# Compressing cached rows with the rows as stationary operand and 256 columns of weights moving, two slots an item

## What is computed

```python
def compress(rows, pe, w1, w2):
    L = rows.shape[1]
    n_cmp = (L - CMP_LEN) // CMP_STRIDE + 1          # CMP_LEN 32, CMP_STRIDE 16
    idx = np.arange(n_cmp)[:, None] * CMP_STRIDE + np.arange(CMP_LEN)[None, :]
    blk = rows[:, idx] + pe[None, None, :, None, :]
    h = jax.nn.gelu(jnp.einsum('bnlgd,lde->bnge', blk, w1))
    return jnp.einsum('bnge,ef->bngf', h, w2)
```

## Time and profile before

| what | value |
|---|---|
| three runs | 2734.03, 2746.77, 2745.37 us, median 2745.37 |
| profiled execution | 2739.43 us, span 2737.6 us |
| mean granted TensorE clock | 0.796 of 2.4 GHz |
| TensorE matmul busy | 2034.7 us (74%) |
| VectorE busy | 1263.8 us (46%) |
| DMA | 963.81 MB, mean 352 GB/s |
| queue of the gathers (software) | 627.05 MB, 56.5% of the 16 engines' span |
| queue of SyncE's loads (hardware) | 332.46 MB, 32.4% |

### The profile page before, as it was taken

The page is one execution under the profiler, slowest core; times in us unless marked ns, Lnnn a source line. Parts: engine busy times, 40 slices in busy tenths (PEclk is TensorE's granted clock), DMA queues, the critical chain, the costliest instruction groups (busy, mean ns, idle before and its releaser), DMA issues.

```text
span 2737.6 us, 30582 instructions
## 1 busy us (share of the span) xinstructions
PE 2034.7 (74%) x10278; PEld 1228.5 (45%) x10278; DVE 1263.8 (46%) x2362; ACT 326.5 (12%) x747; POOL 786.7 (29%) x594
## 2 busy tenths in 40 slices
PE   8999999779989989859998455464544459883334
PEld 5777666434478967647776112211210016540000
DVE  0500112341046775767786354325343454787551
ACT  0000110420021010010010021002010020011011
POOL 0000000000002143433344243225252474346662
PEclk9999999989999989979999766785766555555555
DMA  9789888965327599999999999999999999999997
GB/s 401 294 342 362 350 312 340 384 230 205 122 104 283 178 376 383 370 364 392 387 378 379 351 360 412 406 358 411 389 402 422 422 421 421 422 413 401 422 422 292
DMA packets 213165, 963.81 MB, mean 352 GB/s; under 512 B 23761, under 2 KB 89298, under 8 KB 122258
## 3 DMA queue, kind: packets, MB, share of 16 engines
q0 software_dynamic: 84512, 627.05, 56.5%
q1 hardware_dynamic: 128354, 332.46, 32.4%
q10 hardware_dynamic: 144, 2.36, 0.2%
HBM read 955.28 MB, written 14.88 MB: 354 GB/s over the span
## 4 chain that ended last, share of the span: by engine, by line
PE 46%; DMA 33%; SPq 8%; DVE 7%; issue 4%; POOL 1%; ACT 1%; POOLq 0%; DVEq 0%; ACTq 0%
DMA sb<-in_peer_v,sb 18%; PE bank L891 12%; PE bank L1256 11%; DMA sb<-in_nsa_t 7%; DMA sb<-in_peer_u,sb 6%; SPq L542 5%; PE bank L1481 4%; PE bank L1231 4%; PE bank L1200 4%; SPq L347 2%; DVE sb L2083 2%; PE bank L995 2%; PE bank L955 2%; DMA sb<-in_nsa_v 1%; POOL sb L2176 1%
## 5 line engine op out<-in xcount | busy, mean ns | idle before, releaser
L2083 DVE CUSTOM_DVE_ANT_1 sb<-sb 128x2048 f32<-128x2048 f32 x256 | 585.2, 2292 | 520.4 <-DMA sb<-in_peer_u,sb 516.9
L1481 PE MATMUL bank<-sb 128*32 128x512 f32 x2304 | 478.9, 853 | 417.0 <-DMA sb<-in_peer_v,sb 412.0
L2176 POOL DMA_INDIRECT sb<-in_peer_v,sb x288 | 427.2, 1483 | 659.2 <-PE bank L1481 566.6
L2176 POOL DMA_INDIRECT sb<-in_peer_u,sb x288 | 351.4, 1220 | 633.1 <-DVE sb L2083 366.3
L1256 PE MATMUL bank<-sb 128*128 128x128 f32 x2048 | 467.0, 398 | 60.4 <-DMA sb<-in_nsa_t 59.9
L1256 PEld LDWEIGHTS bank<-sb 128*128 128x128 f32 x2048 | 416.3, 215 | 150.1 <-DMA sb<-in_nsa_t 72.4
L891 PE MATMUL bank<-sb 128*128 128x288 f32 x1408 | 351.0, 409 | 12.1 <-DMA sb<-in_w_in 12.1
L1481 PEld LDWEIGHTS bank<-sb 128*32 128x32 f32 x2304 | 64.9, 126 | 654.7 <-DMA sb<-in_peer_v,sb 594.2
L891 PEld LDWEIGHTS bank<-sb 128*128 128x128 f32 x1408 | 266.4, 191 | 95.6 <-issue 12.2
L865 ACT ACTIVATE sb<-sb 128x32 f32<-128x32 f32 x288 | 85.8, 315 | 814.5 <-PE bank L1481 595.7
L1309 PE MATMUL bank<-sb 128*32 128x512 f32 x128 | 71.1, 722 | 96.7 <-DMA sb<-in_nsa_t 96.7
(11 more groups left out here) (345 smaller groups left out, 1457.4 us busy)
## 6 DMA issues: line engine op xcount, KB each, us to landing
sb<-in_a_k SPq DMA_DIRECT2D x128, 512.0 KB, 6.8
sb<-in_a_v SPq DMA_DIRECT2D x128, 512.0 KB, 6.7
sb<-in_nsa_t SPq DMA_DIRECT2D x384, 128.0 KB, 7.0
sb<-in_w_in SPq DMA_DIRECT2D x44, 1024.0 KB, 9.3
sb<-in_w_out SPq DMA_DIRECT2D x32, 1024.0 KB, 8.9
sb<-in_w_query SPq DMA_DIRECT2D x32, 1024.0 KB, 5.6
sb<-in_nsa_v SPq DMA_DIRECT2D x128, 128.0 KB, 7.9
sb<-in_peer_u,sb POOLq DMA_INDIRECT x288, 15.0
```

Of the source, the lines that this page charges most:

```text
L1481: mm = pe.matmul(bank[g % 2][32 * c:32 * c + 32, :], diag[j % 4], v_ring[j % 4][:, 512 * c:512 * c + 512], start=(s % 32 == 0), stop=(s % ...
L2083: dve.tensor_tensor_reduce(out=u, in0=u, in1=replica(g), scale=1.0, scalar=0.0, op0=ALU.mult, op1=ALU.add, accum_out=act16[:, r % 2, j:j + ...
L2176: pool.indirect_dma_start(rows[j % 4], None, dram[table], bass.IndirectOffsetOnAxis(ap=idx, axis=0)).then_inc(full[j % 4], 16)
```

## The change

An item now takes two ticks. The rows are the stationary operand, both parts of w1 move as one block of 256 columns, and the result (chunks on partitions) is copied out by ScalarE and turned back by two matmuls with the identity, which write into bank 2 shifted by one column for part 1, so that the matmul's accumulation does the addition that VectorE did. All later background work is 34 ticks earlier. The items' banks are 7 and 3 in turn; `cmp_rows` shares the words of `q_t`.

```diff
-TAPS_AT = (2, 54)
-TAPS = {TAPS_AT[kv] + 3 * i + third: (kv, i, third) for kv in range(2) for i in range(2 * NB) for third in range(3)}
+TAPS_AT = (2, 36)
+TAPS = {TAPS_AT[kv] + 2 * i + piece: (kv, i, piece) for kv in range(2) for i in range(2 * NB) for piece in range(2)}
+def item_ticks(after):
+    return {TAPS_AT[kv] + 2 * i + 1 + after: (kv, i) for kv in range(2) for i in range(2 * NB)}
 def stage_ticks(after):
-    return {TAPS_AT[kv] + 6 * b + 5 + after: (kv, b) for kv in range(2) for b in range(NB)}
-CMP_SUM, CMP_EXP, CMP_GELU, CMP_SECOND, CMP_OUT = (stage_ticks(n) for n in (2, 4, 6, 8, 10))
-PICK_AT = 61
-NSA_AT = (104, 138)
-OUT_AT = 179
-QUERY_AT = 212
+    return {TAPS_AT[kv] + 4 * b + 3 + after: (kv, b) for kv in range(2) for b in range(NB)}
+CMP_ROWS, CMP_TURN = item_ticks(1), item_ticks(2)
+CMP_SUM, CMP_EXP, CMP_GELU, CMP_SECOND, CMP_OUT = (stage_ticks(n) for n in (3, 4, 6, 7, 8))
+PICK_AT = 43
+NSA_AT = (70, 104)
+OUT_AT = 145
+QUERY_AT = 178
...
-        HEADS.update({40 + 6 * h: (1, h) for h in range(NH)})
+        HEADS.update({29 + 7 * h: (1, h) for h in range(NH)})
...
-        EXPERTS.update({48 + 12 * p: (1, p) for p in range(4)})
+        EXPERTS.update({37 + 14 * p: (1, p) for p in range(4)})
...
         # SyncE
             for kv in range(2):
-                if kv:
-                    sp.wait_ge(later_used, 16)
-                    sp.dma_start(w1_one, dram["cmp_w1"][:, 1]).then_inc(w1_one_in, 16)
                 for i in range(2 * NB):
                     later_pages(("cmp", kv, i), 8 * i, lambda pg: dram["nsa_t"][bass.ds(pg, 1), kv])
+                    if kv and i == 0:
+                        sp.wait_ge(later_used, 16)
+                        sp.dma_start(w1_one, dram["cmp_w1"][:, 1].rearrange("p (a l) e -> p a l e", a=2)).then_inc(w1_one_in, 16)
...
         # ScalarE
+            def rows_in(kv, i):
+                n = 2 * NB * kv + i
+                act.wait_ge(later_used, later_items.used["cmp", kv, i])
+                if n >= 2:
+                    act.wait_ge(cmp_turned, n - 1)
+                act.activation(cmp_rows[:, n % 2], bank[(7, 3)[n % 2]][:, 0:256], ACT.Copy).then_inc(cmp_rows_in, 1)
...
         # TensorE, taps(kv, i, piece)
-                for n in range(11 * third, min(32, 11 * third + 11)):
-                    part, l = n // 16, n % 16
-                    mm = pe.matmul(ab[:, 256 * part + 128 * half:256 * part + 128 * half + 128], w1_one[:, 16 * part + l, :], rows[:, :, l],
+                    if n >= 2:
+                        pe.wait_ge(cmp_rows_in, n - 1)
+                for l in range(8 * piece, 8 * piece + 8):
+                    mm = pe.matmul(bank[(7, 3)[n % 2]][:, 0:256], rows[:, :, l], w1_one[:, :, l, :],
                                    start=(l == 0), stop=(l == 15), skip_group_check=True)
+            def taps_turn(kv, i):
+                n, b, half = 2 * NB * kv + i, i // 2, i % 2
+                if half == 0 and NB * kv + b:
+                    pe.wait_ge(cmp_sum_out, NB * kv + b)
+                pe.wait_ge(cmp_rows_in, n + 1)
+                for part in range(2):
+                    dst = bank[2][:, 1 - part:257 - part].rearrange("p (g c) -> p g c", g=NG)[:, :, 64 * half:64 * half + 64]
+                    mm = pe.matmul(dst.rearrange("p g (q j) -> p q g j", j=8), cmp_rows[:, n % 2, P * part:P * part + P],
+                                   ident.rearrange("p (q g j) -> p q g j", g=NG, j=8), start=(half == 0 and part == 0), stop=(half == 1 and part == 1),
+                                   skip_group_check=True)
+                mm.then_inc(cmp_turned, 1)
...
         # VectorE, cmp_sums(kv, b)
-                dve.wait_ge(later_used, later_items.used["cmp", kv, 2 * b + 1])
-                if n >= 2:
-                    dve.wait_ge(cmp_mm, n - 1)
-                ch.do(dve.tensor_copy(x_cmp, ab[:, 256:512]))
-                ch.do(dve.tensor_tensor(h[:, :, :, 0:7], a[:, :, :, 0:7], x[:, :, :, 1:8], ALU.add))
-                ch.tell(dve.tensor_tensor(h[:, 0:15, :, 7], a[:, 0:15, :, 7], x[:, 1:16, :, 0], ALU.add), cmp_sum_out, n + 1)
-                ch.do(dve.tensor_scalar(x_cmp, h_cmp[b % 2], pe_bias[:, kv:kv + 1], None, ALU.add))
+                dve.wait_ge(cmp_turned, 2 * n + 2)
+                ch.tell(dve.tensor_scalar(x_cmp, bank[2][:, 1:257], pe_bias[:, kv:kv + 1], None, ALU.add), cmp_sum_out, n + 1)
```

More of the change, by code:

```diff
@@ L427, in hybrid_step @@
         q_t = tail(2, NPROMPT)
+        cmp_rows = q_t
         x_cmp, e_cmp, u_cmp = tail(256), tail(256), tail(256)
@@ L434, in hybrid_step @@
         vcmp = words(AT_PROJ + 4096, NB, NG * P)
-        w1_one = words(AT_T, 32, P)
+        w1_one = words(AT_T, 2, 16, P)
         later_rows = [words(AT_T + 2048 * k, 2048) for k in range(4)]
@@ L465, in hybrid_step @@
         later_used, w1_one_in, cmp_sum_out = sem("later_used"), sem("w1_one_in"), sem("cmp_sum_out")
+        cmp_rows_in, cmp_turned = sem("cmp_rows_in"), sem("cmp_turned")
         v_fresh_in, v_again, saved = sem("v_fresh_in"), sem("v_again"), sem("saved")
@@ L473, in hybrid_step @@
         HEADS = {0: (0, 2), 2: (0, 3), 5: (0, 4), 7: (0, 5), 11: (0, 6), 14: (0, 7)}
-        HEADS.update({40 + 6 * h: (1, h) for h in range(NH)})
+        HEADS.update({29 + 7 * h: (1, h) for h in range(NH)})
         HEADS.update({QUERY_AT + 10 + 4 * h: (2, h) for h in range(NH)})
         EXPERTS = {2: (0, 1), 7: (0, 2), 14: (0, 3)}
-        EXPERTS.update({48 + 12 * p: (1, p) for p in range(4)})
+        EXPERTS.update({37 + 14 * p: (1, p) for p in range(4)})
         EXPERTS.update({QUERY_AT + 15 + 8 * p: (2, p) for p in range(4)})
         GATE_EXPS = {1: (0, 0), 5: (0, 1), 10: (0, 2), 17: (0, 3)}
-        GATE_EXPS.update({50 + 12 * p: (1, p) for p in range(4)})
+        GATE_EXPS.update({39 + 14 * p: (1, p) for p in range(4)})
         GATE_EXPS.update({QUERY_AT + 17 + 8 * p: (2, p) for p in range(4)})
         GATES = {10: (0, 0), 12: (0, 1), 20: (0, 2), 22: (0, 3)}
-        GATES.update({52 + 12 * p: (1, p) for p in range(4)})
+        GATES.update({41 + 14 * p: (1, p) for p in range(4)})
         GATES.update({QUERY_AT + 20 + 8 * p: (2, p) for p in range(4)})
-        EXPERT_FOLDS = {21: (0, 1), 23: (0, 2), 25: (0, 3), 92: (1, 0), 93: (1, 1), 94: (1, 2), 95: (1, 3)}
-        GATE_FOLDS = {24: (0, 1), 26: (0, 2), 28: (0, 3), 96: (1, 0), 97: (1, 1), 98: (1, 2), 99: (1, 3)}
+        EXPERT_FOLDS = {21: (0, 1), 23: (0, 2), 25: (0, 3), 84: (1, 0), 85: (1, 1), 86: (1, 2), 87: (1, 3)}
+        GATE_FOLDS = {24: (0, 1), 26: (0, 2), 28: (0, 3), 88: (1, 0), 89: (1, 1), 90: (1, 2), 91: (1, 3)}
         def replica(g):
@@ L528, in _ @@
             sp.wait_ge(o_a_t, 4)
-            sp.dma_start(w1_one, dram["cmp_w1"][:, 0]).then_inc(w1_one_in, 16)
+            sp.dma_start(w1_one, dram["cmp_w1"][:, 0].rearrange("p (a l) e -> p a l e", a=2)).then_inc(w1_one_in, 16)
             for k in range(16):
@@ L807, in background @@
             def background(t):
+                if t in CMP_ROWS:
+                    rows_in(*CMP_ROWS[t])
                 if t in CMP_EXP:
@@ L1242, in later_arrived, with taps @@
                 return later_rows[later_items.slot[key]]
-            def taps(kv, i, third):
-                b, half = i // 2, i % 2
-                ab = bank[2 + b % 2]
+            def taps(kv, i, piece):
+                n = 2 * NB * kv + i
                 rows = later_rows[later_items.slot["cmp", kv, i]].rearrange("p (c l) -> p c l", l=16)
-                if third == 0:
+                if piece == 0:
                     later_arrived(("cmp", kv, i))
@@ L1251, in taps @@
                         pe.wait_ge(w1_one_in, 16 * (kv + 1))
-                    if half == 0 and NB * kv + b >= 2:
-                        pe.wait_ge(cmp_sum_out, NB * kv + b - 1)
-                for n in range(11 * third, min(32, 11 * third + 11)):
-                    part, l = n // 16, n % 16
-                    mm = pe.matmul(ab[:, 256 * part + 128 * half:256 * part + 128 * half + 128], w1_one[:, 16 * part + l, :], rows[:, :, l],
+                    if n >= 2:
+                        pe.wait_ge(cmp_rows_in, n - 1)
+                for l in range(8 * piece, 8 * piece + 8):
+                    mm = pe.matmul(bank[(7, 3)[n % 2]][:, 0:256], rows[:, :, l], w1_one[:, :, l, :],
                                    start=(l == 0), stop=(l == 15), skip_group_check=True)
-                if third == 2:
+                if piece == 1:
                     mm.then_inc(later_used, 1)
+            def taps_turn(kv, i):
[9 more added lines that the diff above has]
+                mm.then_inc(cmp_turned, 1)
             def second(kv, b):
@@ L1432, in background @@
             def background(t):
+                if t in CMP_TURN:
+                    taps_turn(*CMP_TURN[t])
                 if t in TAPS:
@@ L1917, in cmp_gelu @@
                 dve.wait_ge(gelu_exp, n + 1)
+                if n >= 2:
+                    dve.wait_ge(cmp_mm, n - 1)
```

(2 more changed lines are left out.)

4 lines of the change are left out of this document (removed).

## The result

The kernel is slower by 0.6%: 2754.84 us median (2744.33 to 2769.8) against 2740.22 (2726.15 to 2752.55), 20 runs each, ratio 1.006 with a 95% interval of 1.0041 to 1.0079. The forecast was 2700, faster; the time lies inside the range, 2665 to 2757.

What follows compares the result with a forecast made beforehand. TensorE and DMA were taken as level at 5.97 us a slot, DMA becoming the sole bound. The stage's -36 us and the start made -41, from 2739.4 to 2698, said as 2700; range 2665 to 2757.

Steps and rivals of the forecast that it cites:

- (1): TensorE's taps: 256 columns at about 221 ns a record, so an item falls from 14.5 to 7.1 us.
- D: Rival, chance 0.05: the strided weight load doubles the taps' pass, TensorE takes 8.1 us a slot, +23 us, 2762.
- (2): Turning back on TensorE: two matmuls of 128 columns an item, 4 records, 0.9 us.
- (3): ScalarE's 32 copies of 256 columns: 0.38 us each, 12 us in all, hidden behind TensorE's next taps.
- (7): Head selections moved from every 6 to every 7 slots, later ones 34 earlier: done in time, nothing.
- (4): VectorE's saved work gives nothing except at the start: first sum waits about 10 us, 5 us gained (ends 0 and 16).
- (5): Two slots an item, first value rows to last tap: 49 slots of 6.9 us plus 34 of 5.0, 508 for 544, -36.
- C: Rival, chance 0.12: round trip of two item buffers sets the slots, 9.7 us at worst (+101), likely 8.2, +28, 2767.
- 0.58 us a slot of waits: Compression slots before the change: time above the 5.97 us of TensorE and DMA, when one waited for the other.
- (6): Weights for values: first value item loaded before the last key tap's wait; same bytes, so nothing (ends -8 and +8).

Runs made afterwards that it cites:

- one tick: The changed kernel with a third item buffer and all 16 taps of an item in its second tick: 2690.26 us, ratio 0.9831.
- light first taps: The changed kernel with 2 taps in an item's first tick and 14 in its second instead of 8 and 8: 2735.07 us, ratio 0.999.

## Why the prediction was wrong

The numbers in brackets are the parts of the prediction.

(1) Taps: right. The 16 records of eight matmuls start 3.74 us apart from what follows, 234 ns each, and 48 in a row (from 890.99 to the turn at 901.83 us) 226, against 221 forecast. The strided weight load costs nothing that shows, so D is out; the old form at the new pace, 73 us slower, says the same. (2) The turn: right, 0.55 to 0.65 us an item for 0.9. (3) The copies: right; the turn hardly waited for one. (7) Nothing, as said.

(4) The start: wrong, a term of 5 us gained that measured 9.4 lost. I priced one wait, VectorE's for the first sum, at 10 us. It was 15.03, since the turn of item 1 stood behind item 2's waiting first tap; VectorE's timeline:

```profile
915.76 0.48 DVE L1930 TENSOR_SCALAR sb<-bank,sb 128x256 f32<-128x256 f32 x1 [15.03 <-PE bank L1283]
```

But that wait wasn't the path: with it shortened (copy and turn earlier) the value rows came no sooner. What I didn't count is that at two ticks an item the 18 slots ahead of the value rows hold 8.5 items instead of 5.7. On TensorE that is 67 us instead of 80, but each item from the third on has to be loaded through two buffers: TensorE waits 10.9 us there for cached rows and 4.7 us more for VectorE. At three ticks an item the same form starts 21 us earlier (960.2).

(5) The pace: the step that failed, "I take 6.9". 49 slots measured 7.98 us in the profiled run, which is 53 us more; the start (14.4 from the forecast) and this make 67 of the 68 us between its 2765.9 and the sum's 2698. In the median run the distance is 57, so some 43 are left for the slots, 7.8 us each, if its start is the same.

I took the extra for late items from the stages of selected keys, since TensorE has room to spare there as well. Those stages have four buffers. In its own working of C the prediction had what two buffers do: a period of four slots must hold the use of an item and its landing. It gave the landing at 25.6 us as the worst case and 12% to the rival, "TensorE standing stops the gathers, and the load then speeds up". In the round above the item landed 21.7 us after its buffer came free, at 13% of the bytes, and the use of 11.5 us with it makes the 33.2. The sentence against C held for the other item of the round only (0.90 MB in 4 us): the gathers of four slots had been issued by 1059 and were still landing at 1066.5, so the load that TensorE stood for never sped up. The 25.6 itself was put together wrongly. That "each of SyncE's 128 KB issues is held for 2.3 us" was read from one row; the median issue took 0.33 us, in that stage and in this one. And the 7.0 us added to the 18.6 is already in it: after the change eight pages went out in 4.2 us (1044.9 to 1049.1), and the last one landed 17.4 us after its issue.

C's signs all came: 333 GB/s (under 345), TensorE standing 2.4 us a slot (118.8 of 391.1 us not busy), its decision point at 7.6 us passed, and its likely 8.2 lies close to the 7.98 measured.

What the runs put in place of the 6.9 is two limits, of which the higher holds: two buffers measured 7.98, and with a third one 7.00. One is bytes: 6.4 us at 410 GB/s with two slots an item, 6.0 with three. The other is the round of the two buffers, and here the pace works against itself. In three slots an item, two items leave six slots of other work to hide one landing; in two they leave four, and the landing doesn't shrink as fast (21.7 us where it was 28.7 with three). A third buffer brings the first limit nearer (7.00, with one tick 6.76) or back (6.03 at the old pace).

Why 7.00 and 6.76 stay above 6.4 is not shown. One reason could be the share of a queue: beside queued gathers SyncE's got 13% of the bytes, while a slot at the old pace needs 14% of its bytes from this queue and one at the new pace 20%, which it can have only while gathers have run out. A third buffer with half of the pages on ScalarE's queue would test it; no run has both.

The deeper flaw is that the 34 slots moved were counted as a gain. With their background gone, bytes are moved from one stage to the other and none are saved. At full rate, 49 x 6.4 + 34 x 5.0 is 484 us, and 83 x 5.97 is 496; of these 12 us, 7 are the 2.8 items (2.9 MB) that now come ahead of the value rows. So of my 36 us only 12 at most could come from the pace. The rest had to come out of the 0.58 us a slot of waits (48 us), for which TensorE's room serves at either pace, and to which the new pace adds. The new form at the old pace leaves the ticks alone and gains 18 us in all with two buffers, of which the profile shows 12 in the start and none in the slots, and 55 with three, 31 of them the third buffer's own.

TensorE's clock may have made it worse; no run separates it. After each wait the same 16 records take 5.8 to 6.3 us instead of 3.8, at a granted clock of 0.54 through the wait (1057 to 1068 us), so in part at the lower level of 1.2 GHz. At about 2.2 us a wait and 14 waits in the stage that is some 30 us of TensorE, an estimate; how much of it reached the time is open, and the 19 us of light first taps may hold a part. The prediction allowed up to 3.5 us after a long wait inside its 6.9, but had few such waits in mind. The Trainium skill (TensorE: Matmul & The Clock Gate, "HAM oscillation") warns of just this pattern, bursts of matmuls between waits for DMAs; the trace agrees, with 2.0 to 2.5 us a burst.

That an item is served slowly beside gathers was in the prediction (56 GB/s, 14% of the bytes; measured 51 GB/s, 13%), with the rule of the Trainium skill that each DMA engine takes its queues in turn (DMA: Bandwidth & Descriptors, "Queues, rings and completion order"). The trace agrees: from 1043 to 1066.5 us 1294 packets of SyncE's queue went beside 1089 of the gathers, but of 0.9 KB against 7.3. The run with a second queue bears it out in part: in the same window it shows 920, 1030 and 956 packets of SyncE's, ScalarE's and the gathers' queues, 0.83 and 0.93 MB of cached rows for 1.19, and its longest wait was 9.2 us for 13.6. That step was given as a rival of 12%; it should have been the case.

(6) The weights of the values: not told apart. The longest wait for cached rows was 13.6 us against 20.2, and what it gave is inside S.

## What to carry over

A pace is bounded by the round of its buffers as much as by its engines: before work is packed into fewer slots, add up the use of a buffer, the issue and the landing amid all that is queued beside it, and ask whether the slots of one round are longer. When a form makes an engine cheaper, keep the pace first and look at what is bound then; here the new form alone gave 0.65%, with a third buffer 2.0%, and the faster pace took away from both (0.6% slower than before without that buffer, 1.1% faster with it). A load queued beside larger ones is served by its queue's share, so its landing has to be priced at that share and not at the whole rate. And where bytes bound both stages, slots moved from one to the other gain nothing.

## What the runs showed of the hardware

While gathers were queued, SyncE's queue moved 1.19 of 9.20 MB in 23.5 us (13%, with the DMA engines at 391 GB/s), in 1294 packets of 0.9 KB beside the gathers' 1089 of 7.3 KB. A load of 1.049 MB on it landed 21.7 us after its buffer came free, gathers of the same size 5.7 to 11.0 us after their issue. When the gathers had run out, it moved 0.90 MB in 4 us. The same load split over two queues shortened the longest wait by 4.4 us. Reading the stationary operand of a float32 matmul with a stride of 16 words (128 by 128 out of 2048-word rows) costs no time that shows beside one that lies dense, 226 against 221 ns a record.
